# Gathering expert rows with 0/1 matrices on TensorE, and loading expert weights as whole 2 MB matrices

## The chip, the core and the metric

One core of a Trainium2 chip runs the whole program. The metric is the device time of one execution in microseconds (us), the median of several. A difference of under about 0.2% (4.7 us) can't be told from none here.

## What is computed

Two transformer blocks over one sequence of 512 tokens of width 1024, all in float32. The change lies in the mixture of experts that ends the first block, and in the step from it into the second.

```python
# hf: 512 x 1024, the normalised rows. 64 experts, 2 of them for each token.
g_prob = softmax(hf @ w_group + b_group);  g_w, g_idx = top_k(g_prob, 1)          # one of 8 groups
e_sel = (hf @ w_expert + b_expert) of the chosen group;  top_v, top_i = top_k(e_sel, 2)
gate = g_w * softmax(top_v);  expert_id = g_idx * 8 + top_i
for every expert e, xb = the rows of hf that chose e:
    y = (silu(xb @ w1[e]) * (xb @ w3[e])) @ w2[e]     # w1, w3: 1024 x 512; w2: 512 x 1024
    out[token] += gate * y
x = rms_norm(x + out, final_norm)        # end of block 1
xn = rmsnorm(x, pre_mix_norm)            # start of block 2, then xn @ w_in_2
```

A weight matrix of an expert is 2 MB, an expert is 6.29 MB, and the 64 experts are 402.7 MB.

## The kernel before

Every engine has its own instruction stream, written by hand; semaphores alone tie them together. The large dense products before and after the experts take weights in units of up to 1 MB: SP loads a unit into `raw`, ACT makes its upper part (`w_hi`, `hi_until`, L631), DVE its rest (`w_lo`, `lo_until`, L640), and PE makes three products of them (L562 to L564). `lo_until(v, n)` works off the units up to number n at that place of DVE's stream; `n_first` is the first unit of block 2 (half of the weights of `rq`).

The experts are worked in blocks of up to 32 rows, two blocks to a step of a hardware loop (`u` = 0 and 1, `pe_pair` and its like on the other engines), 32 steps for 64 experts. The ring has 12 buffers of 1 MB, six for each `u`. `load_half` (L1531) fills them from SP: w1 and w3 in halves (k = 0 to 3), then w2 in halves (k = 4, 5). SP waits on `w_used`, which PE raises four times for a block: after each half of the hidden product (L1834) and after each half of the down product (L1843).

The rows travel through DRAM. `dve_route` finds for each token its two experts and its place among an expert's rows (`rank`), POOL scatters token numbers to `slot_ids` with 8 indirect DMAs (L2047) and reads them back, and DVE turns them into two tables of row numbers (L1189 to L1197). Only then does it raise `m_ready`, for which all engines wait ahead of the loop. In the loop POOL gathers the 32 rows of a later block from `h_rows` into `Xe` (L2060), PE transposes them (L1825), ACT copies them into `XTs` (L1661). PE makes `Hb`; DVE copies it to `Hs` (L1985), PE transposes that (L1862), ACT takes silu (L1676), DVE multiplies (L1987), and PE makes the down product. ACT copies it to `y_b` (L1680), and POOL scatters it to `y_rows` (L2065).

After the loop POOL waits for the scatters, and reads `y_rows` back in four DMAs (L2100). DVE adds both expert rows, times their gates, to `x` (L2001). The norm `n3` with its gain follows (L2009), then two `w_lo` (units `n_first` and `n_first` + 1), then the norm `n4` (L2016), and PE turns the rows into columns (`hT3`, L557). DVE's splits of those (L670) come next, then the angles of the rotary embeddings (L1202, and L857 to L867), and then the next `w_lo`.

## Time and profile before

| | us |
|---|---|
| median of 3 runs | 2328.91 (2328.08 to 2332.37) |
| the profiled execution | 2332.82 |
| its span in the trace | 2331.0 |
| PE busy with matmuls in the span | 1789.6 (77%) |
| DVE, ACT, POOL busy | 595.5, 581.9, 171.6 |
| last row of the routing before the loop ends (DVE L1197) | 479.6 |
| hidden product of the first expert starts (PE L1834) | 486.5 |
| down product of the last expert starts (PE L1843) | 1477.4 |
| PE goes on after the experts (L557) | 1521.2 |

The profile cuts the span in 40 slices of 58 us. Its line for DMA gives the busy share of the 16 DMA engines in tenths, its timeline gives start and length of instructions with the idle time ahead of them and what ended it, and its windows add up busy time, granted clock and bytes for a stretch. A busy share over 1 means that transfers of several queues overlapped on an engine.

### The profile page before, as it was taken

How to read it: one execution, taken by the hardware profiler on the slowest of the kernel's cores; microseconds unless marked ns; L12 is line 12 of the kernel's file. 1: busy time of each engine (PE TensorE's matmuls, PEld its weight loads, DVE VectorE, ACT ScalarE, POOL GpSimd, SP SyncE). 2: the span in 40 equal slices, each digit the busy share in tenths (PEclk: the TensorE clock that was granted, in tenths of full speed). 3: DMA queues.
4: the chain of work that ended last, by engine and by line, in shares of the span. 5: the costliest groups of instructions: out<-in, count | busy, mean ns of one | idle time of the engine just before them, and what ended most of it. 6: DMA issues, size and time to landing. Idle time of an engine off the chain costs nothing. (4 is left out here: it accounts for less than half of the span.)

```text
span 2331.0 us, 31203 instructions
## 1 busy us (share of the span) xinstructions
PE 1789.6 (77%) x12156; PEld 1221.0 (52%) x12156; DVE 595.5 (26%) x1085; ACT 581.9 (25%) x978; POOL 171.6 (7%) x290
## 2 busy tenths in 40 slices
PE   6998998656656666666666666379998899998988
PEld 4765787533333333333333333167745678886876
DVE  4437225400000000000000000364365342332145
ACT  3337322111111111111111111232336432221142
POOL 0000000121111111111111111000000000000000
PEclk9999999877787767677777677589989999999999
DMA  5330221669999999999999999522110222323320
GB/s 150 100 100 11 61 102 50 257 233 415 411 412 414 413 411 415 412 414 409 410 412 408 407 404 408 191 73 66 57 36 19 82 73 91 108 81 120 107 73 37
DMA packets 136626, 515.80 MB, mean 221 GB/s; under 512 B 20300, under 2 KB 67848, under 8 KB 86640
## 3 DMA queue, kind: packets, MB, share of 16 engines
q1 hardware_dynamic: 122336, 491.03, 54.3%
q0 software_dynamic: 8272, 17.09, 2.1%
q10 hardware_dynamic: 5952, 6.76, 1.0%
q8 instruction: 47, 0.77, 0.1%
q14 instruction: 19, 0.16, 0.0%
HBM read 510.47 MB, written 12.73 MB: 224 GB/s over the span
## 5 line engine op out<-in xcount | busy, mean ns | idle before, releaser
L1834 PE MATMUL bank<-ring,XTs 128*32 128x256 f32 x4096 | 362.4, 515 | 259.7 <-DMA ring<-in_w 258.7
L1834 PEld LDWEIGHTS bank<-ring,XTs 128*32 128x32 f32 x4096 | 177.9, 142 | 441.7 <-issue 415.6
L562 PE MATMUL bank<-hTh,w_hi 128*128 128x512 f32 (+1 forms) x728 | 290.2, 399 | 8.7 <-DVE w_lo L640 5.8
L640 DVE TENSOR_TENSOR w_lo<-raw,w_hi 128x2048 fp32r<-128x2048 f32 (+3 forms) x84 | 184.3, 2196 | 438.1 <-ACT w_hi L631 438.1
L563 PE MATMUL bank<-hTh,w_lo 128*128 128x512 f32 (+1 forms) x728 | 287.7, 395 | 0.0
L564 PE MATMUL bank<-hTl,w_hi 128*128 128x512 f32 (+1 forms) x728 | 287.1, 394 | 0.0
L1843 PE MATMUL bank<-ring,aT 128*32 128x256 f32 x2048 | 187.9, 522 | 94.0 <-DVE aT L1987 80.6
L1985 DVE COPY Hs<-bank 128x256 f32<-128x256 f32 x64 | 27.2, 424 | 829.8 <-PE bank L1834 829.8
L631 ACT ACTIVATE w_hi<-raw 128x2048 fp32r<-128x2048 f32 (+3 forms) x84 | 153.7, 1832 | 247.2 <-PE bank L564 239.5
L1661 ACT ACTIVATE XTs<-bank 128x256 f32<-128x256 f32 x64 | 24.5, 383 | 635.9 <-PE bank L1825 635.9
L1843 PEld LDWEIGHTS bank<-ring,aT 128*32 128x32 f32 x2048 | 74.1, 142 | 178.9 <-DVE aT L1987 96.0
L562 PEld LDWEIGHTS bank<-hTh,w_hi 128*128 128x128 f32 (+1 forms) x728 | 137.2, 188 | 49.2 <-DVE w_lo L640 12.2
L563 PEld LDWEIGHTS bank<-hTh,w_lo 128*128 128x128 f32 (+1 forms) x728 | 137.3, 189 | 31.3 <-issue 1.0
L564 PEld LDWEIGHTS bank<-hTl,w_hi 128*128 128x128 f32 (+1 forms) x728 | 137.1, 188 | 30.3 <-issue 0.2
L2065 POOL DMA_INDIRECT y_rows<-y_b,scratch x64 | 65.4, 1021 | 798.0 <-ACT y_b L1680 780.4
L562 PE MATMUL bank<-w_hi,ffh 128*128 128x512 f32 x256 | 102.2, 399 | 8.7 <-DVE w_lo L640 7.1
L564 PE MATMUL bank<-w_lo,ffh 128*128 128x512 f32 x256 | 101.6, 397 | 0.0
L562 PE MATMUL bank<-w_hi,hTh 128*128 128x512 f32 (+2 forms) x232 | 83.9, 362 | 6.3 <-DVE hTl L669 6.3
L557 PE MATMUL bank<-cst,arena 128*128 128x128 f32 x148 | 24.4, 342 | 81.6 <-DVE arena L2016 40.2
L1825 PEld LDWEIGHTS bank<-cst,Xe 32*128 32x128 f32 x512 | 61.0, 197 | 44.5 <-issue 44.5
L564 PE MATMUL bank<-w_lo,hTh 128*128 128x512 f32 (+2 forms) x232 | 83.5, 360 | 0.0
L563 PE MATMUL bank<-w_hi,hTl 128*128 128x512 f32 (+2 forms) x232 | 83.5, 360 | 0.0
(343 smaller groups left out, 2045.5 us busy)
## 6 DMA issues: line engine op xcount, KB each, us to landing
ring<-in_w SPq DMA_DIRECT2D x384, 1024.0 KB, 26.9
raw<-in_w_in SPq DMA_DIRECT2D x24, 1024.0 KB, 5.4
raw<-in_w_gate SPq DMA_DIRECT2D x11, 1024.0 KB, 5.4
raw<-in_w_up SPq DMA_DIRECT2D x11, 1024.0 KB, 5.4
raw<-in_w_down SPq DMA_DIRECT2D x11, 1024.0 KB, 4.9
raw<-in_w_out SPq DMA_DIRECT2D x4, 1024.0 KB, 5.0
arena<-y_rows POOLq DMA_DIRECT2D x4, 1024.0 KB, 8.0
raw<-in_w_o SPq DMA_DIRECT2D x4, 1024.0 KB, 4.9
```

Of the source, the lines that this page charges most:

```text
L557: mm = pe.transpose(banks[job.bank][:, P * i:P * (i + 1)], src(i, c), ident)
L562: pe.matmul(dst, left[0], right[0], start=start, stop=False)
L563: pe.matmul(dst, left[1], right[0], start=False, stop=False)
L564: return pe.matmul(dst, left[0], right[1], start=False, stop=stop)
L631: act.activation(w_hi[:, k % PARTS, 0:size], raw[:, k % RAW, 0:size], ACT.Copy).then_inc(hi_made, 1)
L640: v.tensor_tensor(w_lo[:, k % PARTS, 0:size], raw[:, k % RAW, 0:size], w_hi[:, k % PARTS, 0:size].bitcast(F32), ALU.subtract).then_inc(lo_ ...
L1661: act.activation(XTs[u][:, :, :], XTb[:, 0:DC * BLK].rearrange("p (a b) -> p a b", a=DC), ACT.Copy).then_inc(xt_out, 1)
L1825: mm = pe.transpose(XTb[:, BLK * c:BLK * (c + 1)], Xe[u][:, c:D:DC], ident[0:BLK, 0:BLK])
L1834: mm = pe.matmul(Hb[u][BLK * j:BLK * (j + 1), 0:Q], XTs[u][:, 4 * h + c, :], w[:, at_:at_ + Q], start=(h == 0 and c == 0), stop=(h == 1 an ...
L1843: mm = pe.matmul(Yb[u][BLK * j:BLK * (j + 1), 0:Q], aT[:, r, h, :], ring[6 * u + 4 + h][:, at_:at_ + Q], start=(h == 0 and r == 0), stop=( ...
L1985: v.tensor_copy(Hs[:, :], Hb[u][:, 0:Q]).then_inc(h_out, 1)
L2065: pool.indirect_dma_start(y_rows, bass.IndirectOffsetOnAxis(ap=idx_a[u].bitcast(U32), axis=0), y_b[u][:, :], None, bounds_check=last_row, ...
```

## The change

Tokens are chosen and summed on the chip. `tab` (512 x 64 x 2) holds for each token and expert its place among the expert's rows (0 if it has none) and its gate. For a block POOL copies the column of its expert into `sel` and the numbers of its 32 places into `nums`. DVE compares them into a 0/1 matrix `oh` (`choose`), and multiplies it with the gates (`og`, `weigh`). PE multiplies `oh` with the rows `h2`, which stay in SBUF (`gather`, 16 matmuls), ACT copies the result to `xe`, and PE transposes it in two pieces. On the way back PE transposes `og` once for two blocks (`gates_to_rows`), ACT copies it to `g2`, ACT copies the down products to `y2`, and `scatter` multiplies the two for one of 4 tiles of 128 tokens: two matmuls, each over 64 rows of `g2` and `y2` and into its own bank of 128x512. DVE adds the two banks to `x` (`flush`, two adds of 128x512). That goes on one step late, so a step's results are summed in the next.

The weights come in six whole matrices for two blocks. Both halves of the hidden product wait for both w1 and w3, and SP refills them when both halves are done (`w_used` 2), w2 after the whole down product (`w_used` 4). `Hb` and `Yb` have one bank each in place of two.

The 8 indirect DMAs of the routing, `slot_ids`, `h_rows`, `y_rows` and the tables are gone. Behind the loop, the norm `n4` takes its sums from x times the gain of `final_norm` (`xg`), and POOL writes the normed x itself.

```diff
-            def load_half(u, k, expert):
-                m, h = (k % 2, k // 2) if k < 4 else (2, k - 4)
+            def load_matrix(u, m, expert):
...
-                    for k in range(6):
-                        if k in (0, 2, 4, 5):
-                            done = {0: 1, 2: 2, 4: 3, 5: 4}[k]
+                    for m, done in enumerate((2, 2, 4)):
+                        if m != 1:
                             sp.wait_ge(w_used, 2 * STEPS * i + (STEPS * u + done))
-                        load_half(u, k, e)
+                        load_matrix(u, m, e)
...
+            def gather(u):
+                for t in range(NT):
+                    for j in range(4):
+                        mm = pe.matmul(Xp[BLK * j:BLK * (j + 1), :], oh[u][:, t, :], h2[:, t, Q * j:Q * (j + 1)],
+                                       start=(t == 0), stop=(t == NT - 1))
+                mm.then_inc(xe_filled, 1)
...
+            def scatter(i, t):
+                pe.wait_ge(flushed, 4 * i + (t + 5))
+                for n in range(2):
+                    rows_ = slice(2 * BLK * n, 2 * BLK * (n + 1))
+                    mm = pe.matmul(Sb[t % 2][n][:, :], g2[rows_, P * t:P * (t + 1)], y2[rows_, :], start=True, stop=True)
+                mm.then_inc(s_filled, 1)
...
                 for u in range(2):
                     pe.wait_ge(xt_out, 2 * i + (u + 1))
-                    for h in range(2):
-                        for k in (2 * h, 2 * h + 1):
-                            pe.wait_ge(landed[6 * u + k], 16 * i + 16)
-                        hidden(u, h)
+                    for m in range(2):
+                        pe.wait_ge(landed[3 * u + m], 16 * i + 16)
+                    hidden(u, 0)
                     if u == 0 or not last:
-                        pe.wait_ge(gathered[1 - u], 16 * i + (16 if u == 0 else 32))
-                        rows_to_columns(1 - u)
+                        pe.wait_ge(made_oh, 2 * i + (u + 2))
+                        gather(1 - u)
+                    if u == 0:
+                        pe.wait_ge(g_out, i + 1)
+                        pe.wait_ge(y_out, 8 * i + 8)
+                        scatter(i, 0)
+                        scatter(i, 1)
+                    hidden(u, 1)
+                    if u == 0 or not last:
+                        pe.wait_ge(xe_out, 2 * i + (u + 2))
+                        rows_to_columns()
+                    if u == 1:
+                        pe.wait_ge(made_og, 2 * i + 2)
+                        pe.wait_ge(flushed, 4 * i + 10)
+                        gates_to_rows()
...
+                    if u == 0:
+                        scatter(i, 2)
+                        scatter(i, 3)
...
             for i, job in enumerate(J["rank"]):
                 full(v, job)
...
-                    ins = v.tensor_tensor_reduce(junk, banks[job.bank][:, 0:NE], onehot[:, i, k, :], 1.0, 0.0,
-                                                 ALU.mult, ALU.add, rank[:, i, k:k + 1])
...
+                free(v.scalar_tensor_tensor(by_tile[:, i, :], banks[job.bank][:, 0:NE], 1.0, both[:, i, :], ALU.add,
+                                            ALU.mult), job)
+            for k, part in enumerate((masked, e)):
+                chain(v.tensor_tensor(part, onehot[:, :, k, :], gates[:, :, k:k + 1].broadcast_to([P, NT, NE]), ALU.mult))
+            chain(v.tensor_tensor(by_tile[:, NT:2 * NT, :], masked, e, ALU.add))
...
-            v.wait_ge(S("ids_in"), 16)
...
-            chain(v.tensor_scalar(tok_tab[:, :], asg_tab[0:BLK, :], 3, None, ALU.arith_shift_right))
             v.sem_inc(m_ready, 1)
...
+                    if u and last:
+                        hi_at.limit = len(order)
+                        hi_until(act, n_first + 1)
                     act.wait_ge(w_used, 2 * STEPS * i + STEPS * (u + 1))
-                    act.wait_ge(scattered[u], 16 * i + 16)
-                    act.activation(y_b[u][:, :], Yb[u][:, 0:Q], ACT.Copy).then_inc(y_out, 1)
+                    act.wait_ge(s_filled, 4 * i + 4)
+                    for j in range(4):
+                        to = 64 * (j // 2) + BLK * u
+                        act.activation(y2[to:to + BLK, Q * (j % 2):Q * (j % 2 + 1)], Yb[BLK * j:BLK * (j + 1), :],
+                                       ACT.Copy).then_inc(y_out, 1)
...
+            dve_pair(count, True)
             lo_at.limit = len(order)
+            lo_until(v, n_first)
+
+            v.wait_ge(S("w_fin"), 16)
+            for t in range(NT):
+                flush(count + 1, t)
+                v.wait_ge(flushed, 4 * count + (t + 11))
+                v.sem_inc(S("x2pre"), 1)
+                v.tensor_tensor(xg(t), x[:, t, :], gain_fin, ALU.mult).then_inc(S("xg"), 1)
+            dve_rstd(v, chain, "n3", ssq, rstd, NT, D)
...
-            v.sem_inc(S("n3x"), NT)
-            lo_until(v, n_first + 1)
-            dve_rstd(v, chain, "n4", ssq2, rstd2, NT, D)
...
+            v.wait_ge(S("norm_squares"), NORMS["n4"])
...
```

The first place is PE's stream in one block (u = 0) of the loop. Before, from the second half of the hidden product on (`Xe` are the gathered rows, `Hs` the hidden values, `aT` the activated ones):

```order
L1834 MATMUL bank<-ring_77,XTs_88 32x256 x2
L1834 MATMUL bank<-ring_78,XTs_88 32x256 [waits landed3,landed2]
...
L1834 MATMUL bank<-ring_79,XTs_88 32x256 x2
...
L1825 MATMUL bank<-cst,Xe_96 128x32 [waits gathered1]
...
L1862 MATMUL bank<-cst,Hs 128x128 [waits h_out]
...
L1843 MATMUL bank<-ring_80,aT 32x256 [waits landed4,y_out,act_out]
...
L1843 MATMUL bank<-ring_81,aT 32x256 [waits landed5]
...
L1834 MATMUL bank<-ring_82,XTs_89 32x256 [waits landed7,landed6,xt_out]
```

And with the change (`arena` holds the rows `h2`, `oh` is the 0/1 matrix of the next block, `g_90` and `y_91` are the gates and results of the step before; each row of a gather or scatter stands for the rows like it that follow):

```order
L1855 MATMUL bank<-ring_77,XTs_82 32x256 x2
...
L1827 MATMUL bank<-arena,oh_88 32x256 [waits made_oh]
...
L1846 MATMUL bank<-y_91,g_90 128x512 [waits flushed]
...
L1855 MATMUL bank<-ring_76,XTs_82 32x256 x2
...
L1833 MATMUL bank<-cst,xe 128x128 [waits xe_out]
...
L1898 MATMUL bank<-cst,Hs 128x128 [waits h_out]
...
L1864 MATMUL bank<-ring_78,aT 32x256 [waits landed2,y_out,act_out]
...
L1846 MATMUL bank<-y_91,g_90 128x512 [waits flushed]
...
L1855 MATMUL bank<-ring_79,XTs_83 32x256 [waits landed4,landed3,xt_out]
```

The second half of the hidden product and the 8 small transposes that waited for the gather DMA are parted from the first half by 16 matmuls of a gather and two scatters; two more scatters come behind the down product.

The second place is DVE's stream between the end of the experts and the next dense product. Before:

```order
L2001 SCALAR_TENSOR_TENSOR x<-arena,small,x 128x1024 [waits dve_own]
L548 TENSOR_SCALAR small<-small 128x4 [waits norm_squares]
...
L2009 SCALAR_TENSOR_TENSOR x<-x,small,side 128x1024 [waits w_fin,dve_own]
...
L640 TENSOR_TENSOR w_lo<-raw,w_hi 128x2048 [waits hi_made] x2
...
L2016 TENSOR_SCALAR arena<-x,small 128x1024 [waits x2,dve_own]
...
L670 SCALAR_TENSOR_TENSOR hTl<-bank,prm,hTh 128x512 [waits split_hi] x8
L1202 CAST arena<-scratch 128x512 [waits w_pos2]
...
L867 TENSOR_SCALAR tail<-tail 128x512 [waits dve_own]
L640 TENSOR_TENSOR w_lo<-raw,w_hi 128x2048 [waits dve_own,hi_made]
```

With the change (`xg` lies in `arena`):

```order
L640 TENSOR_TENSOR w_lo<-raw,w_hi 128x2048 [waits hi_made]
...
L2046 TENSOR_TENSOR x<-x,bank 128x512 [waits flushed]
...
L2084 TENSOR_TENSOR arena<-x,arena 128x1024 [waits flushed]
...
L548 TENSOR_SCALAR small<-small 128x4 [waits norm_squares]
...
L2097 TENSOR_SCALAR arena<-arena,small 128x1024 [waits xg,dve_own]
...
L670 SCALAR_TENSOR_TENSOR hTl<-bank,prm,hTh 128x512 [waits split_hi] x8
L1203 CAST arena<-scratch 128x512 [waits w_pos2]
...
L867 TENSOR_SCALAR tail<-tail 128x512 [waits dve_own]
L640 TENSOR_TENSOR w_lo<-raw,w_hi 128x2048 [waits dve_own,hi_made]
```

One of the two `w_lo` has moved from ahead of the splits of `hTl` to behind the last angle row (L867).

## Rows read from the trace of the kernel before

**Rows 1.** The page, busy share of the 16 DMA engines in 40 slices

```profile
DMA  5330221669999999999999999522110222323320
```

**Rows 2.** Windows: us, busy (x count) of PE, PEld, DVE, ACT, POOL, clock, DMA, GB/s

```profile
500.00:600.00 100.00, 64.48 (x734) 34.56 (x726) 4.98 (x14) 16.28 (x28) 18.13 (x32) 0.78 1.02 410
```

**Rows 3.** DMA queues from 600 to 1400 us: packets, MB, share of 16 engines

```profile
q1 hardware_dynamic: 44248, 322.23, 98.9%
q0 software_dynamic: 4800, 6.53, 2.4%
```

**Rows 4.** DMA queue from 602 to 611 us, same columns

```profile
q1 hardware_dynamic: 518, 3.80, 101.5%
```

**Rows 5.** The page, DMA issues: count, KB each, us from issue to landing

```profile
ring<-in_w SPq DMA_DIRECT2D x384, 1024.0 KB, 26.9
raw<-in_w_in SPq DMA_DIRECT2D x24, 1024.0 KB, 5.4
```

**Rows 6.** SP's refills at L1531: ns min/median/max, first and last start in us

```profile
L1531 SPq MOVE ring<-in_w x372: 29/29/38, 490.3 to 1448.3; - x186
```

**Rows 7.** Timeline of PE, first experts: start us, us, line, count, idle before, releaser

```profile
486.54 5.98 PE L1834 MATMUL bank<-ring,XTs 128*32 128x256 f32 x64 [0.67 <-ACT XTs L1661]
...
503.41 1.94 PE L1843 MATMUL bank<-ring,aT 128*32 128x256 f32 x32 [0.69 <-DVE aT L1987]
505.16 3.64 PE L1834 MATMUL bank<-ring,XTs 128*32 128x256 f32 x64
...
512.18 3.40 PE L1843 MATMUL bank<-ring,aT 128*32 128x256 f32 x32 [1.95 <-DVE aT L1987]
```

**Rows 8.** Timeline of PE in the attention of block 1

```profile
203.57 1.09 PE L716 MATMUL bank<-cst,scratch 128*128 128x128 f32 x8 [1.01 <-ACT arena L763]
...
205.40 0.70 PE L704 MATMUL bank<-arena 64*128 64x256 f32 x4
```

**Rows 9.** Timeline of DVE, an add of a bank to x

```profile
402.51 0.69 DVE L1968 TENSOR_TENSOR x<-x,bank 128x512 f32<-128x512 f32 x1 [2.11 <-PE bank L564]
```

**Rows 10.** Groups of ACT from 484 to 1480 us, by form: busy us, mean ns, idle before

```profile
L1680 ACT ACTIVATE y_b<-bank 128x256 f32<-128x256 f32 x63 | 24.1, 383 | 228.3 <-PE bank L1843 228.3
```

**Rows 11.** Timeline of DVE, last rows of the routing

```profile
463.75 0.14 DVE L1186 TENSOR_SCALAR small<-small 1x1 int32<-1x1 int32 x1
...
478.93 0.68 DVE L1197 TENSOR_SCALAR scratch<-scratch 32x1024 int32<-32x1024 int32 x1
```

**Rows 12.** Timeline of POOL, first row after the routing

```profile
480.75 0.18 POOL L2069 COPY scratch<-scratch 32x1 int32<-32x1 int32 x1 [7.69 <-issue]
```

**Rows 13.** Timeline of PE, last down product, and the next row after it

```profile
1477.38 3.64 PE L1843 MATMUL bank<-ring,aT 128*32 128x256 f32 x32 [0.69 <-DVE aT L1987]
1521.21 5.80 PE L557 MATMUL bank<-cst,arena 128*128 128x128 f32 x32 [40.19 <-DVE arena L2016]
```

**Rows 14.** Timeline of ACT behind the loop: w_hi, and a sum of squares

```profile
1485.57 3.71 ACT L631 ACTIVATE w_hi<-raw 128x2048 fp32r<-128x2048 f32 x2 [4.10 <-POOLq L2094]
...
1509.89 1.06 ACT L539 ACTIVATE arena<-x 128x1024 f32<-128x1024 f32 x1 [1.56 <-DVE x L2009]
```

**Rows 15.** Timeline of DVE behind the loop

```profile
1494.47 10.15 DVE L2001 SCALAR_TENSOR_TENSOR x<-arena,small,x 128x1024 f32<-128x1024 f32 x8 [17.15 <-DMA arena<-y_rows]
...
1508.57 4.87 DVE L2009 SCALAR_TENSOR_TENSOR x<-x,small,side 128x1024 f32<-128x1024 f32 x4
...
1518.41 2.74 DVE L2016 TENSOR_SCALAR arena<-x,small 128x1024 f32<-128x1024 f32 x4
...
1547.74 0.43 DVE L867 TENSOR_SCALAR tail<-tail 128x512 f32<-128x512 f32 x1
1552.21 2.29 DVE L640 TENSOR_TENSOR w_lo<-raw,w_hi 128x2048 fp32r<-128x2048 f32 x1 [4.04 <-ACT w_hi L631]
```

**Rows 16.** Timeline of PE around the third weight unit of block 2

```profile
1548.59 0.40 PE L564 MATMUL bank<-hTl,w_hi 128*128 128x512 f32 x1
1554.56 0.80 PE L562 MATMUL bank<-hTh,w_hi 128*128 128x512 f32 x1 [5.57 <-DVE w_lo L640]
```

341 lines of the change are left out of this document (168 added, 173 removed).

## The prediction

> **What bounds the kernel now.** I read the slices first, then the windows, the queues, the timelines of PE and DVE at both ends of the loop. The slices show the 16 DMA engines at 9 tenths or more in 16 of 40 slices [rows 1]: that is the expert loop, about 1000 of 2331 us. In a window inside it PE is busy 64.5 of 100 us at a mean granted clock of 0.78, while DMA is busy all the time at 410 GB/s [rows 2]. A 1 MB load lands 26.9 us after its issue, where one issued into an empty queue needs 5.4 [rows 5]: the load queue is never short of work. So the loop lasts as long as its loads. The 12 buffers are full before it starts; the other 62 experts (372 loads, 390.1 MB) are asked for from 490.3 us on [rows 6], and the last down product starts at 1477.4 [rows 13]: 987.1 us. Between 600 and 1400 us the load queue q1 moved 322.2 MB, which is 402.8 GB/s, and beside it POOL's queue q0 (gathers and scatters) 6.5 MB [rows 3]. At 402.8 GB/s the refills take 968.4 us; the other 18.7 us are the landing of the last ones and engines that finish unevenly. On the path lie also the stretch before the first refill and the chain behind the last down product.
>
> **The loop's loads.** The change takes q0's traffic out of the loop and keeps the bytes of q1. In a stretch of 9 us with nothing of q0 in it, q1 alone moved 3.80 MB, 422 GB/s, at 101.5% of 16 engines [rows 4]. That is a direct look at the queue without its neighbour. The price of q0 is bounded from both sides: if it costs only its bytes, q1 rises to what both moved together, (322.2 + 6.5) / 800 = 411 GB/s; if its small packets also disturb, q1 rises to 422. I take 422, since the stretch was measured in the same loop with the same neighbours on PE: 390.1 / 422 = 924.3 us. Of the 18.7 us I keep half, 9.3, for no row says how much of it is unevenness brought by q0 (bounds 0 and 18.7). New: 933.6 us, a gain of **53.5 us** (bounds 19 and 63).
>
> Loads of 2 MB in place of 1 MB I price at nothing: the queue is 26.9 us deep [rows 5], so the start of a load is hidden behind those ahead of it. The Trainium skill (DMA: Bandwidth & Descriptors, the section Measured) says that larger transfers run faster, 341 GB/s at 1 MB and 425 at 16 MB, and puts the ceiling at 435. This trace has 422 with loads of 1 MB already, because many are in flight; by the page's 425 the sum would be 6.5 us lower.
>
> Fewer and later refills: SP now waits for both halves of the hidden product before it refills w1 and w3. The queue still holds the whole other block (6.29 MB, 14.9 us), and the wait is longer by one half product, a gather and two scatters, some 7 us. So the queue doesn't run dry, if PE keeps up.
>
> **Does PE keep up?** The loads of one step of two blocks take 2 x 6.29 / 0.422 = 29.8 us. PE's work for a step, at the full clock: hidden 2 x 3.64 [rows 7] = 7.3. Down 2 x 1.94 [rows 7] = 3.9. A gather has 16 matmuls of the form of a half hidden product, 1.8, twice: 3.6. Transposes of 128x128 came as 4 in 1.09 [rows 8]; there are 2 + 2 + 2 + 2 + 4, so 3.3. A scatter has two matmuls on different halves of the rows; the nearest row is such a couple with 256 columns in place of 512, 0.70 [rows 8]. So it costs 0.7 at least and 1.4 if it grows with the columns; I take 1.4, four times 5.6. Waits for DVE's `aT`, which stay, 0.69 and 1.95 [rows 7]. Sum 26.3 us, 3.5 below 29.8. The 16 small transposes of `Xe` go. DVE adds 8 times 0.69 [rows 9] and ACT 7 copies more of 0.38 or so [rows 10] to a step; both idle for most of 30 us, and their waits reach PE only for tenths, except that the adds of the last two scatters (2.8 us) stand ahead of the next `choose`, which PE's half product and scatter (3.2) cover. So PE stays hidden, with little room.
>
> **Before the first refill.** The last row of the routing ends at 479.6; the row ahead of the wait for `slot_ids` ends at 463.9 [rows 11]. The 15.7 us between (8 scatters, a read back, transposes, tables) go. Added are 3 multiplies or adds of 128x256 and 7 rows of a few numbers, less 8 reductions: 0.14 to 0.69 each by their nearest rows [rows 9, 11], together about 2.1. `m_ready` comes at 466.0. Then before: 1.15 to POOL's first row [rows 12], 486.5 hidden product [rows 7], 6.9 in all. Now: 1.15, POOL's copies 0.4, `choose` 0.3, a gather at the low clock 3.6 (the down product of that clock and length took 3.64) [rows 13], copy, transposes, copy 1.5, hand-overs 0.6: 7.6, so 473.6. The first refill followed 3.8 behind the start of the hidden product. Now it needs both halves (about 4.1, since the gather warms the array), a gather and two scatters (4.6): 482.3. A gain of **8.0 us** (bounds 5 and 10).
>
> **Behind the last load.** Before: from 1477.4 to PE's next row at 1521.2, 43.8 us [rows 13]. In them lie the down product, a scatter DMA, the wait for it, reading back (DVE starts at 1494.5), 10.15 of adding, the norm `n3`, 4.87 of scaling, 2 `w_lo`, `n4` and 2.74 of scaling [rows 15]. Now, counted from the last landing L: ACT first splits two weight units of block 2, which are queued behind the last load. They cost 2.5 each at 422 GB/s and 5.4 with an empty queue [rows 5]; I take 3.5, so L + 7. The second split ends at L + 8.9 (half of 3.71) [rows 14]. Four copies of 0.38: L + 10.4. PE is done by then, though both halves of its last hidden product start only 5 us before L (5.98 from a low clock [rows 7], then down 3.6). First scatter at the low clock, 2.0: L + 12.4. DVE: 4 times two adds of 0.69 and a multiply of 1.22 (a fourth of L2009's 4.87) [rows 15], with ACT's squares beside them: the last square ends at L + 22.9. Root with its table, 2.5: L + 25.4. The squares of `n4`, 4 x 1.2 (1.06 and its read-out) [rows 14], now stand behind it on ACT: L + 30.2. Small rows 1.3, scaling 2.74: **L + 34.3**, a gain of **9.5 us** (bounds 4 and 13, most of it from the two units' arrival).
>
> **A step moved onto the path.** The second of the two `w_lo` stood ahead of the splits of `hTl`, and stands behind all rows of the angles now. Those end at 1548.2 [rows 15]. Before, PE had both units of `rq`, did their four tiles in 22 us (1527.0 to 1549.0), and waited 5.57 us for the third unit, until 1554.6 [rows 13, 16]. Now two tiles take 11 us, and PE waits for the second unit: it is there 2.4 us behind the last angle, on that clock at 1550.6. Then 11 us of work, and 2.4 more at the low clock after the wait: 1564.1 for the start of the third unit, at the full clock. Before it was 1554.6 with those 2.4 us still to pay. A loss of **7.1 us** (bounds 5 and 10). What hid that row before was PE's second couple of tiles; nothing hides it now.
>
> **The sum**, against the profiled execution's own 2332.8: - 53.5 - 8.0 - 9.5 + 7.1 = 2268.9 us. The median of the runs lies 3.9 below that execution, so 2265 us.
>
> **Rivals.** *The rate rises by the bytes only.* At 411 GB/s and with the whole 18.7 us the refills take 967.9 us, 34 more than forecast: **2299 us**. For it: the engines are at 99% with and without q0. Against: [rows 4]. Chance 0.15.
>
> *The unevenness vanishes and larger loads help a little.* 9.3 less, and a few more: **2250 us**. Chance 0.10.
>
> *PE becomes the bound.* Its place is the loop. In the first three blocks there is no wait for loads, and still the down product of the third took 3.40 in place of 1.94 after transposes and a wait of 1.95 [rows 7]. If the array works in a step at the mean clock of 0.78 that it has now [rows 2], its 23.7 us of work become 30.4, and with 2.6 of waits a step takes 33.0 us, 31 steps 1023 us, 89 more than forecast: **2354 us, slower than before**. It begins to bind at 29.8 us a step, and decides against the change above 31.9 us, which is a mean clock under 0.81. Against: a PE that never waits for loads was granted more, and one cold down product a step adds only 1.5. A step of 30 to 31.5 us would give 2270 to 2318. Chances: bound by PE and yet faster 0.10, slower 0.07.
>
> The Trainium skill (TensorE: Matmul & The Clock Gate, HAM oscillation) says that an array that waits for DMA falls back to half its clock and starts each tile cold, and advises long unbroken runs. Whole matrices make one long wait of two short ones, and then a longer run. The trace can't tell which of the two counts more.
>
> *The loads don't speed up at all*, because the 9 us of [rows 4] were a lucky stretch: about 2320 with the two ends. Chance 0.03, and with the loss at the weight unit larger it would be no change.
>
> **Chances and range.** Forecast 0.55, the others as given. The range reaches from the low rival to the bytes-only one with the looser bounds of the ends: 2243 to 2310. A difference of under 0.2% (4.7 us) can't be told from no change. Faster 0.90, same 0.03, slower 0.07.
>
> **What would show it.** In the loop: q1 alone near 422 GB/s with no q0; a step in 29.8 us; PE still waiting for ring loads, if shortly, and busy more than 80 of 100 us. First refill near 482; from the last landing to L557 34 us; a wait of PE of over 10 us for the second `w_lo` of block 2. If PE never waits for a load and SP's queue is empty at times, the third rival holds.

## The result, and the profile after

The changed kernel takes 2256.2 us (median of 4 runs, 2254.5 to 2257.0), the kernel before 2329.3 us in the same comparison: a ratio of 0.9683, with a 95% interval from 0.9667 to 0.9700. The forecast was 2265 us with a range from 2243 to 2310, so the time lies inside it, 9 us under the forecast. The profiled execution took 2254.5 us, its span 2252.7 us.

The page after, the slices (same columns as [rows 1], with the rate beside them):

```profile
DMA  5230121559999999999999999122110223233220
GB/s 155 85 117 15 51 99 56 201 217 426 426 426 427 427 426 426 425 427 428 425 427 426 425 427 415 55 88 65 43 44 29 60 90 104 83 112 112 94 75 38
```

Windows of the loop after (same columns as [rows 2]):

```profile
500.00:600.00 100.00, 78.51 (x993) 41.60 (x984) 26.92 (x62) 29.45 (x60) 2.40 (x14) 0.93 1.01 426
...
1000.00:1100.00 100.00, 77.64 (x956) 40.48 (x952) 26.93 (x62) 26.79 (x55) 2.39 (x14) 0.91 1.01 427
```

DMA queues after, from 600 to 1350 us, and the page's line on the issues (columns of [rows 3] and [rows 5]):

```profile
q1 hardware_dynamic: 28440, 319.74, 100.9%
```

```profile
ring<-in_w SPq DMA_DIRECT2D x192, 2048.0 KB, 19.6
```

The loop is still bound by its loads: the engines are busy without a gap, now with q1 alone. q1 went from 402.8 [rows 3] to 319.74 / 750 = 426 GB/s, and q0 is gone from the list. The share is 100.9% with q1 as the only queue, as it was 101.5% in [rows 4], so a share over 1 doesn't need several queues. POOL's 18 busy us of 100 [rows 2] are 2.4. PE is busy longer, 78 us in place of 64, because gather and scatter are on it, and its granted clock rose from 0.78 to 0.91 to 0.93.

The waits of PE inside the loop after, from 520 to 1380 us: engine, line, what it waited for, us in total, times, longest:

```profile
PE bank L1855 <- DMA ring<-in_w: 107.4, 29, 4.4
PE bank L1864 <- DVE aT L2066: 82.9, 59, 1.7
```

One wait for the ring in each step of two blocks, 3.7 us on average: loads set the pace, and PE is a little ahead of them. A step, from one transposing of `og` (L1838) to the next, takes 29.5 us in the middle of the loop.

The two ends of the loop. First the timeline of PE after, at the start (columns of [rows 7]; the first line is the gather, L1846 the scatter, L1864 the down product):

```profile
470.75 3.64 PE L1827 MATMUL bank<-arena,oh 128*32 128x256 f32 x32 [4.30 <-DVE oh L2028]
...
476.00 1.93 PE L1855 MATMUL bank<-ring,XTs 128*32 128x256 f32 x32 [0.66 <-ACT XTs L1666]
477.72 1.94 PE L1827 MATMUL bank<-arena,oh 128*32 128x256 f32 x32
479.59 1.99 PE L1846 MATMUL bank<-y,g 64*128 64x512 f32 x8
481.51 1.93 PE L1855 MATMUL bank<-ring,XTs 128*32 128x256 f32 x32
...
486.20 1.93 PE L1864 MATMUL bank<-ring,aT 128*32 128x256 f32 x32 [1.70 <-DVE aT L2066]
```

The timeline of SP (first refill), and of PE at the last down product and at the first row behind the chain (which answer [rows 6] and [rows 13]):

```profile
483.65 16.61 SPq L1528 DMA_DIRECT2D ring<-in_w  x6
```

```profile
1403.78 1.93 PE L1864 MATMUL bank<-ring,aT 128*32 128x256 f32 x32 [0.91 <-DVE aT L2066]
...
1439.34 5.87 PE L557 MATMUL bank<-cst,arena 128*128 128x128 f32 x32 [19.38 <-DVE arena L2097]
```

So the spans, 2331.0 and 2252.7, differ by 78.3 us, and they divide like this:

| stretch | before | after | difference |
|---|---|---|---|
| start to first refill | 490.3 | 483.65 | -6.65 |
| first refill to last down product | 987.1 | 920.1 | -67.0 |
| last down product to L557 of block 2 | 43.8 | 35.6 | -8.2 |
| from there to the end | 809.8 | 813.4 | +3.6 |

The medians differ by less, 73.1 us: the profiled execution of before was 3.5 us above its median, that of after 1.7 below.

### The profile page after: what moved, and what is told of

It is laid out like the page before. It is cut to its first block, busy times and chain, and to the rows that moved or that the text cites. A ratio compares the mean times of both kernels' runs of the same rounds, so it can differ in the third digit from the quotient of the medians.

```text
span 2252.7 us, 35882 instructions
## 1 busy us (share of the span) xinstructions
PE 1871.4 (83%) x14468; PEld 1266.2 (56%) x14468; DVE 798.6 (35%) x1526; ACT 694.0 (31%) x1266; POOL 40.8 (2%) x150
## 4 chain that ended last, share of the span: by engine, by line
PE 57%; DMA 27%; DVE 8%; ACT 4%; issue 2%; SPq 1%; ACTq 0%; DVEq 0%; POOLq 0%; POOL 0%
DMA ring<-in_w 26%; PE bank L562 12%; PE bank L563 12%; PE bank L564 12%; PE bank L1855 7%; PE bank L1827 3%; PE bank L1846 3%; DVE w_lo L640 2%; ACT w_hi L631 1%; DMA raw<-in_w_in 1%; PE bank L704 1%; PE bank L557 1%; PE bank L728 1%; PE bank L716 1%; SPq L1528 1%
## 5 line engine op out<-in xcount | busy, mean ns | idle before, releaser
L1855 PE MATMUL bank<-ring,XTs 128*32 128x256 f32 x4096 | 288.9, 430 | 112.1 <-DMA ring<-in_w 111.4
L2046 DVE TENSOR_TENSOR x<-x,bank 128x512 f32<-128x512 f32 x264 | 163.9, 682 | 488.5 <-PE bank L1846 488.5
L1855 PEld LDWEIGHTS bank<-ring,XTs 128*32 128x32 f32 x4096 | 143.1, 121 | 259.6 <-issue 201.8
L1864 PE MATMUL bank<-ring,aT 128*32 128x256 f32 x2048 | 123.8, 382 | 89.0 <-DVE aT L2066 89.0
L1693 ACT ACTIVATE y<-bank 32x256 f32<-32x256 f32 x256 | 96.1, 376 | 220.7 <-PE bank L1846 136.8
L1827 PE MATMUL bank<-arena,oh 128*32 128x256 f32 x2048 | 143.8, 426 | 9.0 <-DVE oh L2028 9.0
L1846 PE MATMUL bank<-y,g 64*128 64x512 f32 x528 | 133.1, 623 | 8.3 <-ACT y L1693 7.0
L1864 PEld LDWEIGHTS bank<-ring,aT 128*32 128x32 f32 x2048 | 66.0, 109 | 128.2 <-DVE aT L2066 59.6
L1827 PEld LDWEIGHTS bank<-arena,oh 128*32 128x32 f32 x2048 | 79.5, 126 | 74.5 <-issue 25.2
L1663 ACT ACTIVATE xe<-bank 128x256 f32<-128x256 f32 x64 | 24.6, 384 | 291.7 <-PE bank L1827 291.7
L1846 PEld LDWEIGHTS bank<-y,g 64*128 64x128 f32 x528 | 45.9, 188 | 68.5 <-issue 65.0
```

Source lines behind the costliest of these rows:

```text
L1663: act.activation(xe[:, :], Xp, ACT.Copy).then_inc(xe_out, 1)
L1693: act.activation(y2[to:to + BLK, Q * (j % 2):Q * (j % 2 + 1)], Yb[BLK * j:BLK * (j + 1), :], ACT.Copy).then_inc(y_out, 1)
L1827: mm = pe.matmul(Xp[BLK * j:BLK * (j + 1), :], oh[u][:, t, :], h2[:, t, Q * j:Q * (j + 1)], start=(t == 0), stop=(t == NT - 1))
L1846: mm = pe.matmul(Sb[t % 2][n][:, :], g2[rows_, P * t:P * (t + 1)], y2[rows_, :], start=True, stop=True)
L1855: mm = pe.matmul(Hb[BLK * j:BLK * (j + 1), :], XTs[u][:, 4 * (c % 2) + 2 * h + c // 2, :], w[:, at_:at_ + Q], start=(h == 0 and c == 0), s ...
L1864: mm = pe.matmul(Yb[BLK * j:BLK * (j + 1), :], aT[:, r, h, :], ring[3 * u + 2][:, at_:at_ + Q], start=(h == 0 and r == 0), stop=(h == 1 an ...
```

## Experiments on the loop: where 67 us came from

Three things differ in the loop's traffic: the size of the transfers, the small traffic on POOL's queue, and the kind of that traffic. Four kernels put them back one upon another, starting from the changed kernel.

**Transfers of 1 MB again.**

```diff
-                sp.dma_start(dst, src).then_inc(landed[3 * u + m], 16)
+                for k in range(2):
+                    if m < 2:
+                        sp.dma_start(dst[:, 4 * k:4 * k + 4, :], src[:, 4 * k:4 * k + 4, :]).then_inc(landed[3 * u + m], 16)
+                    else:
+                        sp.dma_start(dst[:, k, :], src[:, k, :]).then_inc(landed[3 * u + m], 16)
...
-                    pe.wait_ge(landed[3 * u + m], 16 * i + 16)
+                    pe.wait_ge(landed[3 * u + m], 32 * i + 32)
```

> The changed kernel, but each whole matrix is fetched by two transfers of 1 MB (pieces of 8 KB instead of 16 KB), with the two issued together and waited for together; nothing else differs. Theory (the size of a piece sets part of the rate): the old kernel's queue moved 422 GB/s with 8 KB pieces where nothing else ran, the changed one 426 to 427 GB/s with 16 KB pieces; the loop's 390.1 MB then take 924 instead of 915 us, so the time is 9 us above the changed kernel, about 2265 us, and the queue shows 422 GB/s. Rival (the 1 to 1.2 per cent came from the traffic beside it being gone, and piece size is nothing): within 2 us of the changed kernel, 2256 us, 426 GB/s. The prediction priced the larger pieces at nothing, which is this rival.

Measured: 2263.9 us (2262.2 to 2264.8), 7.6 above the changed kernel, and the loop 929.1 us in place of 920.1. Queue q1 from 600 to 1350 us:

```profile
q1 hardware_dynamic: 43453, 316.48, 101.3%
```

That is 422 GB/s, the rate of [rows 4]. The engines are as busy as with whole matrices, with half as many packets again. In the changed kernel's trace, over the same 750 us, a packet of 8 KB takes 314 ns on average and one of 16 KB 615, which is 307 for 8 KB. (Only `w1` and `w3` have pieces of 16 KB; `w2` kept 8 KB. The expectation speaks as if all had.) The theory holds: size is worth 9 us of the loop, and the prediction had it at nothing.

**Small traffic again, in plain transfers.**

```diff
+            def extra():
+                pool.dma_start(av(12288, D)[0:16, :], a["x"][0, 0:16, :]).then_inc(S("q0_in"), 16)
+                pool.dma_start(q0_rows, h2[0:64, 0, 0:Q]).then_inc(S("q0_out"), 16)
...
+                    pool.wait_ge(S("q0_in"), 32 * i + 16 * (u + 1))
+                    pool.wait_ge(S("q0_out"), 32 * i + 16 * (u + 1))
                     pool.wait_ge(made_og, 2 * i + (u + 1))
...
+                    extra()
```

> The changed kernel with small traffic put back on GpSimd's queue beside the loads: for each block one transfer in of 16 rows of 4 KB and one out of 64 rows of 1 KB, into and from places that nothing uses, about what the old kernel's gather and scatter moved for a block (6.5 MB in 800 us). No work of the kernel waits for it before the loop's end. Theory (the load queue loses far more than its bytes to such traffic, since small packets stand in the same engines): the queue's rate falls from 426 to about 408 GB/s, the loop's loads take 956 us instead of 915, and the time rises by some 35 to 45 us to about 2295 us. Rival (only bytes count: 131 KB beside 6.29 MB a block is 2 per cent): 418 GB/s, plus 18 us, 2274 us. Second rival (the old loss was from the refill's waits, not the traffic): no change, 2256 us.

Measured: 2302.9 us (2298.4 to 2304.5), 46.7 above the changed kernel; loop 969.1 us. The queues from 600 to 1350 us:

```profile
q1 hardware_dynamic: 27050, 303.97, 98.4%
q0 software_dynamic: 3072, 6.30, 2.5%
```

q1 fell from 426 to 405 GB/s, 5%, for a neighbour that has 2% of the bytes. The sum of both is 414, well below 426, so the rival that counts bytes is out. Half of the 5% is in the shares: q0's packets hold the engines for 2.5% of the time. The other half is in q1's own packets: those of 8 KB took 335 ns on average against 314 without q0, those of 16 KB 618 against 615. The effect is a little above the 35 to 45 us expected. POOL does wait for the transfers of the block before, but that holds nothing up: PE's waits for `oh`, which POOL's next copies feed, are 3.9 us in all from 520 to 1380 us, 4.4 in the changed kernel. So traffic that holds nobody up by a wait costs more than all else that the change did.

**Both.**

> Both of the two edits above: whole matrices fetched in two transfers of 1 MB, and the small traffic put back beside them. Theory (the two effects add and make up the old kernel's loop): the queue falls to what the old kernel had in the loop, about 403 GB/s, the loop's loads take 965 to 970 us against 920, and the time is about 2303 us; the old kernel's loop took 987, and the remaining 18 us are the unevenness of its refills by halves. Rival (the effects overlap, being the same cost of many packets): no more than the small traffic alone.

Measured: 2307.7 us (2305.4 to 2308.5), loop 976.3 us, q1 at 301.59 / 750 = 402 GB/s, the old kernel's 402.8 [rows 3]:

```profile
q1 hardware_dynamic: 41411, 301.59, 98.9%
q0 software_dynamic: 3072, 6.30, 2.5%
```

The two add in part: 9 and 49 us of loop alone, 56 together. The rate is the old kernel's, and still the loop is 11 us shorter than its 987.1. So the remainder is not in the rate. In the old kernel it is at the loop's end. Windows of the old kernel, from 1452 to 1464 us (the next to last column is the share of the 16 engines):

```profile
1452.00:1456.00 4.00, 3.10 (x32) 1.24 (x24) 0.00 (x0) 0.00 (x0) 0.00 (x0) 0.50 1.02 423
1456.00:1460.00 4.00, 3.33 (x32) 1.57 (x32) 0.00 (x0) 0.00 (x0) 0.00 (x0) 0.50 0.53 219
1460.00:1464.00 4.00, 3.31 (x46) 2.20 (x42) 0.71 (x2) 0.66 (x2) 0.00 (x0) 0.91 0.26 107
```

SP's last refill was issued at 1448.3 [rows 6], and the last two halves of hidden products waited for the ring until 1466.6 and 1471.8 us. At 1460 us three quarters of the engines had nothing left to carry, while a few still had their part of those loads; a load has landed when its last part has. This is the unevenness that the prediction put at 18.7 us and kept half of. In the kernel with plain small traffic the windows from 1440 to 1460 us show no share under 1.01. That alone doesn't say that its ring loads end evenly, for there SP has issued block 2's first weight units at 1451.1 us, while the last ring load lands at 1457.5 (old kernel: 1464.4, and 1476.7). The landings further down say it without them.

**The small traffic by indirect transfers.** Halves as above, and (`idx_i` holds row numbers that are made once, ahead of the loop):

```diff
-                pool.dma_start(av(12288, D)[0:16, :], a["x"][0, 0:16, :]).then_inc(S("q0_in"), 16)
-                pool.dma_start(q0_rows, h2[0:64, 0, 0:Q]).then_inc(S("q0_out"), 16)
+                pool.indirect_dma_start(av(12288, D)[0:BLK, :], None, a["x"][0], bass.IndirectOffsetOnAxis(
+                    ap=idx_i[0:BLK, :].bitcast(U32), axis=0), bounds_check=in_bound, oob_is_err=False).then_inc(S("q0_in"), 16)
+                pool.indirect_dma_start(q0_rows, bass.IndirectOffsetOnAxis(ap=idx_i.bitcast(U32), axis=0), h2[:, 0, 0:Q],
+                                        None, bounds_check=out_bound, oob_is_err=False).then_inc(S("q0_out"), 16)
```

> As the kernel with halves and small traffic, but the small traffic goes by indirect transfers as in the old kernel: for each block 16 of 32 rows of 4 KB gathered and 64 of 128 rows of 1 KB scattered, the other rows out of bounds. The plain version took 976 us from the first refill to the last down product, the old kernel 987; the old kernel's trace shows that from 1457 us on only some 4 of the 16 DMA engines still carried ring packets (0.53 and 0.26 of the engines' time at 1456 to 1464 us), and the last half landed at 1471.7 us, while the plain version and the changed kernel end with all engines busy. Theory (indirect transfers with rows left out load the 16 engines unevenly, so that a few lag): the loop takes 985 to 990 us, with the engines' share below 0.6 for about 10 us before the last weights land, and the time is about 2319 us. Rival (the lag comes from the old kernel's refill by halves on TensorE's progress, not from the traffic's kind): 976 us, 2308 us, engines busy to the end.

Measured: 2319.9 us (2317.8 to 2323.1); the loop 988.0 us, against the old kernel's 987.1. The queues from 600 to 1350 us, and two windows near the end of the loop:

```profile
q1 hardware_dynamic: 41053, 298.94, 98.2%
q0 software_dynamic: 4512, 6.18, 2.4%
```

```profile
1456.00:1460.00 4.00, 4.00 (x51) 1.63 (x40) 2.36 (x4) 0.38 (x1) 0.00 (x0) 1.00 1.00 416
1460.00:1464.00 4.00, 3.13 (x44) 1.62 (x40) 1.23 (x5) 0.66 (x2) 0.00 (x0) 1.00 0.60 250
```

Some of the thinning is back, though the refills are those of the kernel with plain small traffic: that much comes from the kind of traffic, not from the old way of refilling. It is shorter than in the old kernel (about 4 us below full before block 2's units, issued at 1464.0, join in; 10 were expected), and the rate is lower, 398.6 GB/s against 402.

How much is back, the landings show. A ring load raises its semaphore 16 times as its parts land, and the trace has the time of each. From the first to the last of the 16, in us:

| kernel | mean, loads issued 580 to 680 us | mean, issued 1280 to 1380 us | the last ring load |
|---|---|---|---|
| before | 7.2 | 20.0 | 19.7 |
| changed | 1.6 | 1.9 | 2.3 |
| halves | 1.9 | 1.8 | 1.8 |
| halves and plain small traffic | 2.2 | 3.4 | 4.3 |
| halves and indirect small traffic | 4.9 | 5.9 | 8.6 |

In the old kernel the parts drift apart through the whole loop, and only its end makes one pay: 12 parts of the last load had landed by 1460.7 us, the last at 1476.7. The indirect traffic of the experiment brings back a part of that drift, and it does so from the start.

The loop divided into the refills' bytes at the rate of q1 (from 600 to 1350 us; before, [rows 3]) and the rest:

| kernel | loop | at q1's rate | rest |
|---|---|---|---|
| changed | 920.1 | 915.0 | 5.1 |
| halves | 929.1 | 924.4 | 4.7 |
| with plain small traffic | 976.3 | 970.0 | 6.3 |
| with it indirect | 988.0 | 978.6 | 9.4 |
| before | 987.1 | 968.4 | 18.7 |

So of the 67 us **9 are for the size of the transfers and 47 for the small traffic**; these two are measured, and give back the old kernel's rate. The other 11 are the old loop's end. Making the small traffic indirect costs 12 us in the experiment, but 8.6 of them by a lower rate, which the old kernel doesn't have, and 3.1 at the end. So the agreement of 988.0 with 987.1 is in good part chance. Some 9 us of the old loop's end no experiment reproduces: whether they come from the real row numbers, from refills on each half product, or from something else isn't shown. Nor does the trace name the engines that carry the rows of an indirect transfer, so why they are uneven stays open.

## Experiments on the margin of TensorE

```diff
-                        gather(1 - u)
+                        for _ in range(3):
+                            gather(1 - u, _ == 2)
```

(Only the last of the three raises `xe_filled`; the kernel with two has 2 and 1 in these places.)

> The changed kernel with each gather product inside the loop made three times over instead of once (same result, 32 more TensorE instructions of 256 columns for a block, 3.9 us for a block and 7.7 us for a step of two blocks at full clock). It measures how far TensorE is from becoming the bound. Theory (loads set the loop, and TensorE has 3.7 us of slack in a step, as its waits for the ring say): 7.7 less 3.7 is 4.0 us for each of 31 steps, plus 124 us, about 2380 us, with TensorE never waiting for the ring. Rival (the granted clock rises as TensorE is busier, so that the work already there gets shorter): plus 60 to 100 us. Rival (TensorE was the bound already, in part): plus 7.7 for each step, 240 us, 2495 us.

> The changed kernel with each gather product inside the loop made twice instead of once (16 more TensorE instructions for a block, 3.9 us for a step at full clock). Theory (TensorE has 3.7 us of slack in a step of two blocks): 0.2 us for each of 31 steps, plus 0 to 10 us, 2256 to 2266 us, while the waits of TensorE for the ring go from 107 us to nearly nothing. Rival (no slack: the waits for the ring come from uneven arrival, and TensorE's own work sets part of the steps): plus 40 us or more.

Measured, with three gathers: 2295.5 us (2293.6 to 2297.4), 39 above the changed kernel, not 124. With two: 2258.7 us (2253.7 to 2259.8), and 921.1 us for the loop. Windows from 600 to 700 us, two gathers and then three:

```profile
600.00:700.00 100.00, 87.10 (x1201) 47.44 (x1194) 26.04 (x60) 26.34 (x56) 2.06 (x12) 0.95 1.01 426
```

```profile
600.00:700.00 100.00, 90.55 (x1341) 51.91 (x1334) 25.10 (x57) 24.81 (x52) 2.05 (x12) 0.98 0.98 409
```

With three, PE is the bound. Its waits from 520 to 1380 us have no line for the ring any more (the queue's rate falls to 409, since loads now wait for PE):

```profile
PE bank L1865 <- DVE aT L2068: 79.0, 56, 1.7
PE bank L1900 <- DVE Hs L2062: 5.0, 28, 0.2
...
```

What was added is less than the 7.7 us that the expectation has, for a gather right behind another adds less than the 1.93 us of one alone:

```profile
906.88 5.39 PE L1827 MATMUL bank<-arena,oh 128*32 128x256 f32 x96
```

Two gathers more took 5.39 - 1.93 = 3.46 us, so a step got 6.9 us more work. The loop grew by 43.4 us, 1.4 for each of 31 steps, so by the loop's totals the margin is 5.5 us. Most steps with three gathers, from one transposing of `og` to the next, take 30.5 us, at the full clock; less 6.9, PE's own step is 23.6, where the changed kernel's takes 29.5; by single steps the margin is 5.9. The wait for the ring shows only 3.7 us of the margin, and most of the rest is the lower clock: the changed kernel's hidden products take 433 ns in the mean, with two gathers 387, with three 381. I had read the margin off the wait alone, as the theories for three gathers, for two, and for the order of `h2` further down do, and so missed by a factor of three (with 6.9 in place of 7.7 us it would have been 99 us for 39). With two gathers the time is inside the expected range; the waits for the ring are 33.2 us, not nearly nothing. The rival that the clock rises with the work is the right one in kind, yet at 60 to 100 us was not bold enough.

The same lines from the groups of PE, 520 to 1380 us (busy us, mean ns | idle before), of the changed kernel, then of the one with two gathers:

```profile
L1855 PE MATMUL bank<-ring,XTs 128*32 128x256 f32 x3712 | 264.6, 433 | 107.4 <-DMA ring<-in_w 107.4
```

```profile
L1856 PE MATMUL bank<-ring,XTs 128*32 128x256 f32 x3756 | 231.2, 387 | 33.2 <-DMA ring<-in_w 33.2
```

## Experiments on the two ends

**The moved `w_lo`.**

```diff
-            lo_until(v, n_first)
+            lo_until(v, n_first + 1)
```

> The changed kernel, with one instruction of VectorE moved back: the low half of block 2's second projection unit is made behind the loop's last block, ahead of the scatter's sums, instead of behind the angles. VectorE stands idle there for 4.6 us and the operation takes 2.29. Theory (TensorE's third unit waits for it in the changed kernel, 7.1 us by the prediction, 7.4 us by the trace): minus 7 us, about 2249 us, and the stretch from the first product of block 2 to its rotation back from 65.2 to 57.8 us. Rival (later waits take it back, as 2.8 us of it were made good further on in the changed kernel): minus 3 to 4 us. Rival (the operation delays the scatter's sums): no gain.

Measured: 2249.7 us (2246.2 to 2254.1), 6.5 under the changed kernel. PE after, at the second weight unit of block 2, and in the experiment at the third:

```profile
1468.82 0.80 PE L562 MATMUL bank<-hTh,w_hi 128*128 128x512 f32 x1 [12.61 <-DVE w_lo L640]
```

```profile
1471.29 0.80 PE L562 MATMUL bank<-hTh,w_hi 128*128 128x512 f32 x1 [5.34 <-DVE w_lo L640]
```

The wait of 12.61 us is gone, and PE waits 5.34 for the third unit, as before (5.57, [rows 16]). From the first L557 of block 2 to its first rotation the trace has 57.8 us before, 65.2 after, 58.3 here. So the move costs 7 us and nothing takes it back; the rest of block 2 is 748 to 749 us in both kernels.

**GpSimd beside VectorE.**

```diff
             pool.wait_ge(S("r3"), 1)
+            pool.wait_ge(S("xn4"), NT)
             for i in range(NT):
-                pool.wait_ge(S("xg"), i + 1)
```

> The changed kernel, with GpSimd's four scalings of the residual rows (12.1 us from 1428.06 us on) held back until VectorE has made its own four of the normalised rows. Theory (GpSimd and VectorE slow each other while both read and write the on-chip memory, and these four took VectorE 4.41 us beside GpSimd against 2.74 in the old kernel): minus 1.7 to 3 us, about 2254 us. Rival (VectorE's four are longer for where their operands lie, not for the neighbour): no change. Rival (the rows that GpSimd makes are wanted sooner than the profile shows): plus up to 4 us.

Measured: 2251.6 us (2249.9 to 2257.0), 4.6 less, from runs that spread over 7; the profiled one is the slowest, 2257.0. The stretch itself is sharper: from the last down product to L557 32.6 us in place of 35.6. VectorE in the changed kernel, with POOL's row beside it, and then in the experiment:

```profile
1432.74 1.02 DVE L2091 TENSOR_SCALAR small<-small 128x4 f32<-128x4 f32 x1
...
1434.24 0.60 DVE L2094 TENSOR_TENSOR small<-small 128x4 f32<-128x4 f32 x1
```

```profile
1428.06 12.11 POOL L2150 TENSOR_SCALAR x<-arena,small 128x1024 f32<-128x1024 f32 x4 [63.08 <-DVEq L2086]
```

```profile
1434.86 0.17 DVE L2091 TENSOR_SCALAR small<-small 128x4 f32<-128x4 f32 x1
...
1435.52 0.16 DVE L2094 TENSOR_TENSOR small<-small 128x4 f32<-128x4 f32 x1
1435.71 2.74 DVE L2097 TENSOR_SCALAR arena<-arena,small 128x1024 f32<-128x1024 f32 x4
```

Of the five rows on 4 numbers here one took 1.02 us beside POOL and 0.17 without, one 0.60 and 0.16, and three were no longer beside POOL than without it (0.16 to 0.18). The four scalings took 4.41 beside it and are 2.74 again, the duration of [rows 15]. In the old kernel POOL had no work there.

A part of the gain is only moved. POOL's scalings now run beside the first rows of the angles. Here is one of these rows, in the experiment and then in the changed kernel:

```profile
1447.48 1.22 DVE L1204 COPY scratch<-arena 128x512 f32<-128x512 f32 x1
```

```profile
1447.72 0.43 DVE L1204 COPY scratch<-arena 128x512 f32<-128x512 f32 x1
```

Three of them (L1203, L1204, L859) take 2.1 us more together, PE waits 14.7 us for the `w_lo` behind the angles in place of 12.6, and from L557 to the first rotation the trace has 66.3 us in place of 65.2.

**The order of the rows `h2`.** The change has DVE write them permuted, reading `x` with a stride of 8 elements. The experiment keeps plain rows and lets PE's gather read with the stride:

```diff
-                v.scalar_tensor_tensor(h2[:, i, :].rearrange("q (c p) -> q c p", c=DC), by_eighths(x[:, i, :]),
-                                       rstd[:, i:i + 1], by_eighths(row_gain), ALU.mult, ALU.mult).then_inc(S("h2"), 1)
+                v.scalar_tensor_tensor(h2[:, i, :], x[:, i, :], rstd[:, i:i + 1], row_gain, ALU.mult,
+                                       ALU.mult).then_inc(S("h2"), 1)
...
-                        mm = pe.matmul(Xp[BLK * j:BLK * (j + 1), :], oh[u][:, t, :], h2[:, t, Q * j:Q * (j + 1)],
+                        mm = pe.matmul(Xp[BLK * j:BLK * (j + 1), :], oh[u][:, t, :],
+                                       by_eighths(h2[:, t, :])[:, 2 * j:2 * j + 2, :],
```

> The changed kernel, with the normalised rows kept in their natural order: VectorE's four scalings read and write plain rows (4.87 us in the old kernel against 7.95 in the changed one, which reads with a stride of 32 bytes), and TensorE's gather reads the rows with that stride instead; the router's weights are laid out as in the old kernel. Theory (TensorE reads a strided operand at the same rate): minus 3.1 us at the start and nothing in the loop, about 2253 us. Rival (the strided reading slows the gather): the 16 products of a gather take longer than 1.93 us; up to 1.85 us a gather more are hidden behind the loads' slack of 3.7 us a step, beyond that each us costs 62 us in all.

Measured: 2256.6 us (2253.2 to 2258.9), no gain. The routing is done 3.1 us sooner (its last row at 465.83 in place of 468.93), but the gather takes twice as long, 3.90 in place of 1.94 us:

```profile
475.11 3.90 PE L1827 MATMUL bank<-arena,oh 128*32 128x256 f32 x32
```

That is at the full clock; the first gather of all, at a granted clock of 0.50, took 3.89 in place of 3.64. One such gather at the full clock stands ahead of the first refill and takes 2 us back there (483.0 against 483.65); the loop is 1.3 us longer, 921.4. What is left is less than a comparison can tell. The gathers in the loop are hidden, as with two gathers for one.

**The repairs together**, measured on one chip beside the changed kernel itself:

> The changed kernel with both small repairs: the low half of block 2's second unit made behind the loop's last block, and GpSimd's four residual scalings held back until VectorE's normalised rows are made. Theory (the two are in different places of one chain and add): 6.5 and 2.9 us off, about 2247 us, ratio to the old kernel 0.9645. Rival (the second is given back behind, as its own profile's later part was 3 us longer): 2250 us.

> The kernel before this one with one further edit: VectorE's four scalings of the normalised rows read plain rows and write the permuted order (stride of 512 bytes on the way out) instead of reading with a stride of 32 bytes; TensorE's gather stays as in the changed kernel. Theory (the 7.95 us against 4.87 come from the strided reading of two operands): 4.87 us again, 3.1 us off, about 2244 us. Rival (any stride slows the engine, whichever side it is on): 7.95 us or more, no gain.

> The changed kernel itself once more, as the yardstick for the two kernels beside it, on the same chip: 2256 us, and ratios to it rather than across calls. Where its own profile differs from the first one, that is what a single profile's parts are uncertain by: about 2 us in the part before the loop is expected, under 1 us in the loop.

| kernel | median us | runs | ratio to before, 95% interval |
|---|---|---|---|
| changed, again | 2255.7 | 2253.2 to 2257.8 | 0.9678, 0.9663 to 0.9692 |
| both repairs | 2246.9 | 2245.4 to 2249.3 | 0.9642, 0.9628 to 0.9656 |
| both, and the strided side swapped | 2246.0 | 2243.4 to 2247.5 | 0.9637, 0.9623 to 0.9651 |

Together they bring 8.8 us, from runs that don't overlap. The theory said 9.4 for the sum, and the medians of the two alone 11.1. The trace has 32.7 us from the last down product to L557 (3 less than changed) and 59.1 from there to the rotation, 0.8 more than with the moved `w_lo` alone. The swap of sides shortens DVE's four rows only from 7.95 to 7.32 us (the changed kernel, then the swap):

```profile
429.19 7.95 DVE L2019 SCALAR_TENSOR_TENSOR arena<-x,small,side 128x1024 f32<-128x1024 f32 x4 [0.26 <-DVE small L550]
```

```profile
427.84 7.32 DVE L2019 SCALAR_TENSOR_TENSOR arena<-x,small,side 128x1024 f32<-128x1024 f32 x4 [0.27 <-DVE small L550]
```

So it isn't the reading alone: writing with a stride of 512 bytes costs nearly as much as reading two operands with one of 32. Its 0.9 us of the median lies within the spread.

The changed kernel's second profile repeats the first: 919.9 us of loop, 35.6 and 813.6 us behind it. The part ahead of the loop is the least steady one: with the same code there, the routing ended between 467.2 and 471.1 us in the other kernels. The difference of 6.65 us at the start is known to about 2 us.

## Why the prediction was right, and where it was off

**What bounds the loop, and the side:** right. Loads set it before and after, q1 sped up once q0 was gone, and the queue of whole matrices never ran dry.

**The rate.** Predicted 422 GB/s from nine microseconds without q0 [rows 4], against 411 if only bytes count; the rate with 1 MB transfers is exactly 422, over 750 us. The part of the sum for it was 44 us (968.4 less 924.3); putting the small traffic back cost 47. The step that was mis-sized is the one priced at nothing: larger transfers brought 9 us. The argument given, that a deep queue hides the start of a load, is true of a load's start and says nothing of what each packet costs on an engine. The figures of the Trainium skill (DMA: Bandwidth & Descriptors, Measured) pointed the right way: it has large transfers ahead of small ones, and with its 425 the sum would have been 6.5 us lower. The trace after has 426 to 427. Its 341 for 1 MB doesn't hold in a full queue: the 422 measured here decides.

**The unevenness.** 9.3 of 18.7 us were kept. After, 390.1 MB at 426.3 GB/s take 915.0 of 920.1 us, so 5.1 are left. I had said that no row tells how much is q0's. The landings above tell some of it: with q0's traffic gone the parts of a load land within 2 us, not 20, yet the experiments give back only about 4 of the 13.6 us by which the rest shrank. They also correct my reading of [rows 5]. The 26.9 us are the landing of a load's last part. Late in the old loop its first part landed 7 us after the issue, little above the 5.4 of an empty queue; the queue was deep only for the slowest parts.

Together the loop gained 67.0, not 53.5: 13.5 us more, 9 from size and 4 from unevenness. That is the step that failed most, and the lowest rival (unevenness vanishes, larger loads help) had its mechanism, though with 2250 us it went too far in the total.

**PE keeps up:** right, and with more room than I gave it. I had 26.3 us for a step; it is 23.6. A scatter was priced at 1.4 us, bounded by 0.7 from the row of 256 columns [rows 8]; two took 1.92 from start to start, so one costs 1.0, between the bounds, and four 1.8 us less than in my sum. Transposes cost 2.4, not 3.3. These two terms make up the difference. The rival in which the array works at the mean clock of 0.78 fell for the reason that was written against it: busier, it was granted 0.91, and in the experiments up to 0.98. (Its 2354 us also leaves out the 9.3 us of unevenness that its other figures, 31.9 us a step and 2270 to 2318, keep; on their footing it would be 2364.) The margin was elastic in a way that I hadn't seen. A half product that follows a wait for the ring still starts cold, 3.29 us in place of 1.93:

```profile
1382.98 3.29 PE L1855 MATMUL bank<-ring,XTs 128*32 128x256 f32 x32 [3.24 <-DMA ring<-in_w]
```

One such wait a step costs PE about 1.4 us, inside its margin. The Trainium skill (TensorE: Matmul & The Clock Gate, HAM oscillation) has that cold start, and its advice of long runs agrees with the higher mean clock of this trace.

**Before the first refill.** Predicted 482.3, measured 483.65; a gain of 6.65 for 8.0. The parts: from the routing's end to the first hidden product 6.9 us, not 7.6; from there to the refill 7.65, not 8.7, since the array was at full clock at once. Against these stands what I didn't price at all: the permuting read in `h2`, 7.95 us for 4.87, ahead of the routing. I took it for a change of addresses.

**Behind the last load.** Predicted a gain of 9.5, measured 8.2. The two weight units arrived at 1406.1 and 1409.1, the second 5.3 us behind the start of the last down product. Copies, sums and squares came out about as priced. The 3 us of POOL beside DVE were missing from the sum: the change lets POOL begin its scalings just when DVE has its last ones. I had read of DVE's rows in the old kernel, and not asked what POOL does there in the new.

**The moved `w_lo`:** predicted +7.1, measured +7.4, and taken back for 7. The right mechanism at the right size. The end as a whole lost only 3.6 against the old kernel's profile. Of the difference, 2.8 us are one place, where the old kernel's profiled execution had the low clock:

```profile
1700.15 7.19 PE L1025 MATMUL bank<-arena,cst 4*128 4x512 f32 x8 [2.53 <-DVE arena L1257]
```

```profile
1625.26 4.40 PE L1033 MATMUL bank<-arena,cst 4*128 4x512 f32 x8 [2.53 <-DVE arena L1258]
```

The granted clock there is 0.50 in the first and 0.72 in the second. That execution also was 3.5 us above the median, so I take this for its luck and not an effect of the change. With one profile of the old kernel that isn't shown, but kernels with the changed one's code in this place have the same row at 4.53 us (the second profile of the changed kernel), 5.75 (the moved `w_lo`) and 7.19 (the delayed scalings).

**The sum.** Against the old kernel's own time the changed one came out 14.4 us shorter than forecast: 13.5 more gained in the loop, 1.3 less at the start, 1.3 less behind it, 3.5 less lost in block 2. I had taken off 3.9 for where the old profile lies above its median, and the new one lies 1.7 below its own: 14.4 - 3.9 - 1.7 = 8.8 us, which is how far the forecast of 2265 is from 2256.2.

## What to carry over

A queue that is never empty can still be slow: look for other traffic on the same engines and price it by a stretch without it, not by its bytes; 2% of the bytes cost 5% of the rate, and the same bytes by indirect transfers another 12 us. Look at the first part of a load to land as well as the last: the two drifted 20 us apart here, and the busy share didn't show it. When work moves to an engine that now waits, don't read its margin off the waits alone, since a part of the slack hides in the granted clock (3.7 us of waits, 5.5 of margin); repeat a known piece of work until the time moves. And of each step that a change moves, ask what else now runs at that time (POOL beside DVE: 3 us) and what no longer hides it (7 us): both took a line or two to repair, and gave 9 us.

## What the runs showed that I had not expected

- In a full queue, transfers of 2 MB, two thirds of them in pieces of 16 KB, ran at 426 GB/s; of 1 MB in pieces of 8 KB at 422.
- In the old loop the first and the last part of a 1 MB load landed 7 us apart early on and 20 us apart late; in the changed one about 2 us apart throughout.
- Beside a POOL row of 12.11 us on 128x1024 tiles, one of five DVE rows on 128x4 took 1.02 us in place of 0.17, and the four scalings 4.41 in place of 2.74.
- DVE's product of two operands, 128x1024 four times: 4.87 us plain, 7.95 read with a stride of 32 bytes, 7.32 written with one of 512.
- A PE product whose moving operand is read with a stride of 32 bytes took twice as long at the full clock, 3.90 us for 1.94, and hardly longer at the half one, 3.89 for 3.64.
- 6.9 us more of PE's work in each step, where its waits for loads were 3.7 us, lengthened the step by 1.4 us only, while the granted clock rose from 0.91 to 0.98.
